# 104 gathered tokens spread over all partitions in place of 72, and 416 dense columns in place of 448, in a one-core decoder layer

## The reference

```
q = einsum('pd,dk->pk', xb, w_q)                 # 8 heads, two halves of 128
s = einsum('phcd,hcnd->phcn', q, keys)
s1, i1 = top_k(s[:, :, 0], 16); s2, i2 = top_k(s[:, :, 1], 16)
cand = s1[..., :, None] + s2[..., None, :]       # 16 x 16 for each head
top_s, top_pos = top_k(cand, 16)                 # 16 experts for each head
gate = softmax(top_s)                            # 8 x 16 = 128 gates for each token
a = gelu(einsum('pd,ped->pe', xb, u_tab[eidx]))
out = einsum('pe,ped->pd', gate * a, v_tab[eidx])
```

## Time and profile before

| | us |
|---|---|
| three runs | 2015.57, 2026.8, 2033.81 |
| median | 2026.8 |
| the profiled execution, its own time | 2021.1 |
| its span | 2018.5 |
| PE busy / POOL busy / DVE busy / ACT busy | 1891.0 / 1240.6 / 1114.7 / 607.5 |
| mean granted clock of TensorE | 0.967 |

### The profile page before, as it was taken

How to read it: one execution, slowest core, us unless ns; L and a number is a source line. 1 busy time by engine, 2 the same in 40 slices (tenths; PEclk the granted TensorE clock), 3 DMA queues, 4 the chain that set the end, 5 groups by cost and what they waited for, 6 DMA issues and landing times.

```text
span 2018.5 us, 31683 instructions
## 1 busy us (share of the span) xinstructions
PE 1891.0 (94%) x12867; PEld 1784.1 (88%) x12867; DVE 1114.7 (55%) x2280; ACT 607.5 (30%) x770; POOL 1240.6 (61%) x668
## 2 busy tenths in 40 slices
PE   5999996999999999999899999999899989889996
PEld 4889864969999999999899999998888888879896
DVE  4622646176477466667832122256576666567676
ACT  5212322232233323233332222232222223223232
POOL 0230100003777888888888887368888888888850
PEclk9999997999999999999999999999999999989997
DMA  7422395574356575766576666777878878878781
GB/s 259 177 84 95 110 345 156 178 246 141 64 127 143 113 156 100 154 123 131 120 186 141 143 138 134 215 243 242 256 219 260 242 226 253 241 214 271 234 240 48
DMA packets 210418, 361.75 MB, mean 179 GB/s; under 512 B 93969, under 2 KB 143121, under 8 KB 203233
## 3 DMA queue, kind: packets, MB, share of 16 engines
q1 hardware_dynamic: 136096, 318.76, 49.1%
q0 software_dynamic: 74176, 40.97, 15.2%
HBM read 291.45 MB, written 68.16 MB: 178 GB/s over the span
## 4 chain that ended last, share of the span: by engine, by line
PE 36%; POOL 21%; DVE 7%; issue 6%; DMA 3%; ACT 0%; another core or an unknown queue 0%; DVEq 0%; SPq 0%; ACTq 0%
PE ps L1469 29%; POOL ag L1637 12%; POOL qp L1644 9%; PE ps L1492 6%; DMA qp<-vtab,row 3%; DVE ul L1680 1%; PE ps L1455 1%; PE ps L1434 1%; DVE topi L135 0%; DVE h L214 0%; DVE h L228 0%; DVE h L223 0%; DVE pick L218 0%; DVE pick L235 0%; DVE h L207 0%
## 5 line engine op out<-in xcount | busy, mean ns | idle before, releaser
L100 POOL DMA_INDIRECT gates_dram<-gate,where x384 | 655.4, 1707 | 335.5 <-DVE where L254 193.0
L1492 PE MATMUL ps<-cl,uh 128*128 128x448 f32 x1024 | 380.2, 371 | 44.2 <-DVE ul L1680 43.3
L1469 PE MATMUL ps<-hl,uh 128*128 128x260 f32 x2048 | 415.7, 284 | 2.3 <-DVE ul L1680 2.3
L1469 PE MATMUL ps<-hh,ul 128*128 128x260 f32 x2048 | 414.0, 284 | 0.0
L1469 PE MATMUL ps<-hh,uh 128*128 128x260 f32 x2048 | 413.2, 283 | 0.0
L1492 PE MATMUL ps<-ch,ul 128*128 128x448 f32 x1024 | 377.6, 369 | 0.0
L1492 PE MATMUL ps<-ch,uh 128*128 128x448 f32 x1024 | 377.2, 368 | 0.0
L1680 DVE TENSOR_TENSOR ul<-us,uh 128x1024 fp32r<-128x1024 f32 x132 | 161.2, 1224 | 351.8 <-issue 244.2
L1637 POOL DMA_INDIRECT ag<-ahead_dram,where x128 | 275.5, 2153 | 72.8 <-issue 38.8
L1469 PEld LDWEIGHTS ps<-hl,uh 128*128 128x128 f32 x2048 | 316.9, 189 | 3.2 <-DVE ul L1680 2.9
L1469 PEld LDWEIGHTS ps<-hh,ul 128*128 128x128 f32 x2048 | 316.9, 189 | 0.0
(11 more groups left out here) (222 smaller groups left out, 2341.7 us busy)
## 6 DMA issues: line engine op xcount, KB each, us to landing
us<-utab SPq DMA_DIRECT2D x128, 512.0 KB
pairs<-vtab SPq DMA_DIRECT2D x124, 512.0 KB
ahead_dram<-a SPq DMA_DIRECT2D x128, 224.0 KB
qp<-ahead_dram SPq DMA_DIRECT2D x64, 448.0 KB
gt<-gates_dram SPq DMA_DIRECT2D x64, 448.0 KB
wr<-w_ada SPq DMA_DIRECT2D x24, 1024.0 KB, 6.0
gates_dram<-blank SPq DMA_DIRECT2D x24, 1024.0 KB, 8.8
wr<-w_in SPq DMA_DIRECT2D x14, 1024.0 KB, 4.8
```

Source lines behind the costliest of these rows:

```text
L100: nc.gpsimd.indirect_dma_start(out=io["gates"].rearrange("g p c a t -> (g p c a t)").unsqueeze(1), out_offset=bass.IndirectOffsetOnAxis(ap ...
L1469: last = nc.tensor.matmul(out[:, half, :], w, r[:, k, half * TH:(half + 1) * TH], start=(k == 0 and q == 0), stop=(k == KD - 1 and q == 2))
L1492: last = nc.tensor.matmul(ps[:, k, 0:ND], w, r[:, n % NL, :], start=(n == 0 and q == 0), stop=(n == NK - 1 and q == 2))
```

## The change

- The last tile begins at 416: `EDGES` is 0, 128, 256, 384, 416, 520. So `ND` is 416, `TG` is 104, and the fourth tile has 32 tokens in place of 64.
- A gathered token's 128 experts are spread over several partitions. The 104 tokens are three groups: the last 8 tokens (the samples) over 16 partitions each, 32 tokens over 4 each, 64 tokens over 2 each. Every group fills 128 partitions, with 8, 32 and 64 choices for each partition, 104 choices in all. There are therefore 104 pairs of indirect DMAs with 128 rows in place of 128 pairs with 72 rows, and 104 sums of 128 x 1024.
- The offsets, rows and gates of the last tile are brought into that layout through DRAM: SP writes them with nine strided DMAs (`pack`, ahead of block 85 of the first stage) and reads them back with one (`packed_back`); GpSimd waits for it ahead of its gathers.
- `fg` has three parts, one for each group. The samples' part is folded from 128 partitions to 8 by four pairs of a DMA on SP and an addition on DVE (`fold`, at blocks 30 to 44). The partial sums of the two prompt groups are added by 8 products each with a 0/1 matrix (`gathered_sums`, float32) right into the columns 416 to 511 of the eight banks, after blocks 70 and 126. The first product of each bank is 512 wide to clear them.
- `GCH`, the number of activations fetched ahead, is 8 in place of 16. `summed` now places the last sum at block 123.
- The samples' squares and norm move from the end into blocks 46 and 50. Behind the last block the norm and the residual run over 512 columns in place of 448, and the separate pieces for the 64 gathered prompt tokens go.

```diff
-EDGES = (0, 128, 256, 384, 448, T)
+EDGES = (0, 128, 256, 384, 416, T)
...
+GROUPS = ((96, 8), (64, 32), (0, 64))
...
-    TD = ND // 4
+    TD = SEQ // 4
...
-    GCH = 16
+    GCH = 8
...
+    GROUP_AT = [sum(n for _, n in GROUPS[:g]) for g in range(len(GROUPS) + 1)]
+    PACK_AT, PACKED_AT = 84, 88
+    FOLDS = (64, 32, 16, 8)
+    FOLD_AT, FOLD_EVERY = 30, 4
+    SAMPLES_AT = FOLD_AT + FOLD_EVERY * len(FOLDS)
+    TURN_AT = 70
...
-        return 0 if n < G0 else min(HK, -(-(n - G0 + 1) * HK // (NK - G0 - 1)))
+        return 0 if n < G0 else min(TG, -(-(n - G0 + 1) * TG // (NK - G0 - 4)))
...
+                def pack():
+
+                    sp.wait_ge(pick_ok, picked(TILES - 1))
+                    for a_, src in enumerate((where[:, TILES - 1].bitcast(F32), row[:].bitcast(F32),
+                                              gate[:, TILES - 1])):
+                        for g, (first, n) in enumerate(GROUPS):
+                            sp.dma_start(packing[a_].rearrange("(h t) s -> t h s", t=n)
+                                         [:, :, GROUP_AT[g]:GROUP_AT[g + 1]],
+                                         src[first:first + n].rearrange("t (h s) -> t h s", s=n))\
+                                .then_inc(packed_out, 16)
...
+                def gathered_sums(g):
+
+                    first, n = GROUPS[g]
+                    pe.wait_ge(fg_ok, GROUP_AT[g + 1])
+                    pe.wait_ge(chosen_ok, 1)
+                    for k in range(KD):
+                        nc.tensor.matmul(ps[:, k, ND + first:ND + first + n], fg[:, g, k * P:(k + 1) * P],
+                                         chosen[:, first:first + n], start=False, stop=False)
...
+                            whole = n == 0 and q == 0
+                            columns = slice(0, SEQ if whole else ND)
+                            last = nc.tensor.matmul(ps[:, k, columns], w, r[:, n % NL, columns],
+                                                    start=whole, stop=(n == NK - 1 and q == 2))
...
-                pool.wait_ge(pick_ok, picked(TILES - 1))
+                pool.wait_ge(packed_in, 16)
                 pool.wait_ge(g_ok, BATCHES)
                 for m in range(NK - NA, NK):
                     pool.wait_ge(*stored(m))
-                for r in range(-GCH, HK):
-                    if r + GCH < HK:
+                for r in range(-GCH, TG):
+                    if r + GCH < TG:
                         at = r + GCH
                         nc.gpsimd.indirect_dma_start(
                             out=ag[:, at:at + 1], out_offset=None, in_=words,
-                            in_offset=bass.IndirectOffsetOnAxis(ap=where[0:TG, TILES - 1, at:at + 1], axis=0))\
+                            in_offset=bass.IndirectOffsetOnAxis(ap=packed_choice[:, 0, at:at + 1].bitcast(U32), axis=0))\
                             .then_inc(ag_in[at // GCH], 16)
...
                         nc.gpsimd.indirect_dma_start(
                             out=vg[:, r % NG, :], out_offset=None, in_=values,
-                            in_offset=bass.IndirectOffsetOnAxis(ap=row[0:TG, r:r + 1], axis=0))\
+                            in_offset=bass.IndirectOffsetOnAxis(ap=packed_choice[:, 1, r:r + 1].bitcast(U32), axis=0))\
                             .then_inc(vg_in[r % NG], 16)
...
-                    nc.vector.scalar_tensor_tensor(fg[:], vg[:, r % NG, :], ag[:, r:r + 1], fg[:],
+                    sums_of = fg[:, group_of(r), :]
+                    nc.vector.scalar_tensor_tensor(sums_of, vg[:, r % NG, :], ag[:, r:r + 1], sums_of,
                                                    ALU.mult, ALU.add).then_inc(fg_ok, 1)
+
+                def fold(n):
+
+                    w = FOLDS[n]
+                    dve.wait_ge(fold_in, 16 * (n + 1))
+                    nc.vector.tensor_tensor(fg[0:w, 0, :], fg[0:w, 0, :], folded[0:w], ALU.add).then_inc(fold_ok, 1)
```

More of the change, by code:

```diff
@@ L44 @@
 NGRP = NK // GB
-AHEAD = NK
+AHEAD = NK + 1
 CLEARS = 24
@@ L1244, in summed, with group_of @@
     def summed(n):
-        return 0 if n < G0 else min(HK, -(-(n - G0 + 1) * HK // (NK - G0 - 1)))
+        return 0 if n < G0 else min(TG, -(-(n - G0 + 1) * TG // (NK - G0 - 4)))
+    def group_of(r):
+        return next(g for g in range(len(GROUPS)) if r < GROUP_AT[g + 1])
     stack, early = ExitStack(), ExitStack()
@@ L1313, in peer_stage @@
         cl_ok = sem("cl_ok")
-        ag_in = [sem(f"ag_in{n}") for n in range(HK // GCH)]
+        ag_in = [sem(f"ag_in{n}") for n in range(TG // GCH)]
+        packed_out, packed_in = sem("packed_out"), sem("packed_in")
+        fold_in, fold_ok, chosen_ok = sem("fold_in"), sem("fold_ok"), sem("chosen_ok")
         vg_in = [sem(f"vg_in{n}") for n in range(NG)]
@@ L1381, in coefficients @@
                             sp.wait_ge(scattered[i], 16 * HK)
-                        for c in range(2):
-                            sp.wait_ge(kept[c], 16 * (ST // CH // 2))
+                        for c in range(ST // CH):
+                            sp.wait_ge(kept[c % 2], 16 * (c // 2 + 1))
                     if q >= NV:
@@ L1497, in _ @@
                         last.then_inc(w_mm, 1)
+                    if n == TURN_AT:
+                        gathered_sums(1)
+                    if n == NK - 2:
+                        gathered_sums(2)
                 pe.wait_ge(fn_ok, 1)
-                pe.wait_ge(f_ok, 2)
-                pe.wait_ge(fsq_ok, 2)
+                pe.wait_ge(f_ok, 1)
+                pe.wait_ge(fsq_ok, 1)
                 for k in range(KD):
[L1503 to L1506, removed]
+                    last = nc.tensor.transpose(ps[:, 0, k * NS:(k + 1) * NS], sample_rows[:, k * P:(k + 1) * P],
+                                               ident[0:NS, 0:NS])
                 last.then_inc(ft_mm, 1)
                 pe.wait_ge(sum_ok, 1)
-                pe.wait_ge(fs_ok, 1)
-                for c in range(ND // TD):
+                pe.wait_ge(f_ok, 2)
+                for c in range(SEQ // TD):
                     last = nc.tensor.matmul(ps[0:TD, 1, c:c + 1], squares[:, 0, c * TD:(c + 1) * TD], ones[:, 0:1],
@@ L1756, in _ @@
                     if n == 0:
-                        dve.wait_ge(kept[0], 16 * (ST // CH // 2))
-                        dve.wait_ge(kept[1], 16 * (ST // CH // 2))
+                        for c in range(ST // CH):
+                            dve.wait_ge(kept[c % 2], 16 * (c // 2 + 1))
                         coefficients(0)
                         coefficients(1)
+                        nc.vector.tensor_scalar(cl[:, 0, ND:SEQ], ident[:, 0:SEQ - ND], 0.0, None, ALU.mult)
                         low_coefficients(0)
-                        nc.vector.memset(fg[:], 0.0)
+                    if 0 < n <= len(GROUPS):
+                        nc.vector.memset(fg[:, n - 1], 0.0)
+                    if n == len(GROUPS) + 1:
+                        for first, columns in GROUPS[1:]:
+                            last = nc.vector.tensor_reduce(chosen[:, first:first + columns],
+                                                           ident.rearrange("p (h t) -> p t h", t=columns), AX.X,
+                                                           ALU.add)
+                        last.then_inc(chosen_ok, 1)
                     if 0 <= n < NK - LEAD:
```

105 lines of the change are left out of this document (65 added, 40 removed).

## The result

| us | before | after |
|---|---|---|
| median, beside each other on one chip | 2022.3 (2015.57 to 2033.81) | 1917.49 (1916.59 to 1918.47) |
| ratio, 95% interval | | 0.9476 (0.9428 to 0.9525) |
| span of the profiled execution | 2018.5 | 1914.8 |
| first stage ends | 1315.3 | 1305.1 |
| second stage, to the end of its last product | 680.5 | 587.5 |

The kernel is 5.2% faster; 1.2% slower was forecast. The spans differ by 103.7 us: 10.2 less ahead of the second stage, 93.0 less in it, 0.5 less behind it.

What follows compares the result with a forecast made beforehand. It took gathers, admitted only in DVE's pauses, to set the second stage's pace, not PE. First stage -10, second stage +34, 0/1 products +2 on 2021.1 gave 2047; plus 5.7 to the median, stated as 2052, range 1966 to 2114.

Steps and rivals of the forecast that it cites:

- First stage, -10: First stage: halving the fourth tile's 16 batches saves 7 us, and a late batch that goes saves 3.
- PE's pace, 0.1864 a product: Second stage: 416 columns take 0.1864 us a product, 4.48 a block for 4.80, 41 us less if PE sets the pace.
- rival C: Second stage: PE stays the bound and DVE's gap does not matter, 128 x 4.48 us; total 1921, chance 0.07.
- The gather of 128 rows at 1.55 us: GpSimd, second stage: a 128-row gather takes 1.55 us, taken from the scatter, between bounds 0.94 and 1.67.
- rival B: Second stage: rows nearly free on GpSimd, 0.94 us a gather, 5.7 us a sum; total 1983, chance 0.20.
- The gap of 1.06 us: Second stage: at PE's new pace DVE's idle gap in a block with a sum is 1.06 us.
- One DMA passes, not 1.79: Second stage: indirect DMAs get on only in DVE's gaps; one passes a block where 1.79 are needed.
- the 87 sums at 6.5 us: Second stage: once the lead is used up, 87 sums wait for rows at 6.5 us each, 566 us in all.
- The number of DMAs a block: Second stage: the indirect DMAs needed a block fall from 2.15 to 1.79.
- Rival B's bytes, 5.2 us a block at 271 GB/s: Second stage: DMA engines must move 1.42 MB a block, allowing no faster than 5.2 us a block, 5.8 a sum.
- Rival D: Second stage: GpSimd keeps DVE out for a whole 128-row gather, at least 7.4 us a sum; total 2130, chance 0.06.
- 0/1 products, 2: PE, second stage: 16 products with the 0/1 matrices, half in DVE's shadow and half on the path, add 2 us.

Runs made afterwards that it cites:

- e12: Kernel before with 104 of its 128 sums (72 partitions) and 416 columns in all second-stage blocks but first and last: 1925.28 us, ratio 0.953.
- e8: Kernel before with only the second stage narrowed to 416 columns, first and last block excepted; 128 sums over 72 partitions: 2015.32 us, ratio 0.9977.
- e7: Kernel before with only 104 of its 128 sums and their gathers done; 72 partitions, 448 columns: 1959.39 us, ratio 0.9715.
- e4: Kernel before with its DVE sums over 128 partitions in place of 72 (extra weights 0), gathers still 72 rows: 1962.3 us, ratio 0.9696.
- e11: Kernel before with its 128 sums over 128 partitions and 416 columns in all blocks but first and last; 72-row gathers: 1952.15 us, ratio 0.9642.
- e14: Kernel before with 128 sums over 128 partitions, 416 columns in inner blocks, and v_tab gathers of 128 rows: 1920.39 us, ratio 0.9497.

## Why the prediction was wrong, step by step

- **First stage, -10:** right, 10.2.
- **PE's pace, 0.1864 a product:** 2% too fast. From 1631.01 on, 56 blocks took 255.37 us, 0.190 a product and 4.56 a block in place of 4.48. The 0.200 for 448 columns was read from two starts; over the last 480 products of the kernel before it is 97.87/480 = 0.204. For the whole stage rival C had 573 + 10 = 583, and it took 587.5.
- **The gather of 128 rows at 1.55 us:** wrong, 0.94. The scatter of the earlier trace rows was the nearest row and the wrong kind of row. In the forecast's own sum it is worth 69 us (2052 against rival B's 1983), about half of the miss; the other 66 are the next step but one. No run has a gather of 1.55, so what that would have cost with the gate as it is stays open.
- **The gap of 1.06 us:** right (1.05 in e12).
- **"One DMA passes, not 1.79":** this is the step that failed, and the forecast held it for a gather of 0.94 us too. It rests on "an indirect DMA gets on only when DVE pauses", which was false: a DMA can get in between two DVE instructions that follow back to back, and the trace of before has cases (the DMA of 1422.61 above). In e12 a second DMA that starts just behind the gap, while DVE is in `cl`, gets in at the end of `cl`; in the changed kernel 81 of the 87 that stand behind the coefficients get in there, with no gap either. Two pass in a block, so "PE's pace can therefore not be held" falls, and with it the 10 blocks of lead and the 87 sums at 6.5 us: 715 for the second stage, where 587.5 came and DVE waited for no row.
- **The number of DMAs a block:** the forecast had it, 2.15 to 1.79, and gave it too little. The room at PE's pace is near two: e8, which needs more, gains nothing from its columns; e7, which needs less, gains 58 us. A GpSimd that has fallen behind gets less, as most of its DMAs that stand long are held (32 of 36 at the boundary behind `cl`).
- **The sum, 1.28 us at either width:** right for DVE. That its width decides about GpSimd's DMAs was in no step. It is a second way to the same gain (e4), which the changed kernel has but does not need.
- **Rival B's bytes, 5.2 us a block at 271 GB/s:** wrong as a ceiling. That rate belonged to gathers of 72 rows (e11 sits on it, 32 us above e14); with 128 the engines moved 313 to 344. Whether a row's time to landing L stayed as it was, no wait after shows: DVE waits for none.
- **Rival D:** falls; no gather kept DVE out, and e14's DVE does 128 wide sums at PE's pace.
- **0/1 products, 2:** 1.71 and 1.73, 3.4 in all, as both turns lie on the path. **Behind the last block, 0 within 2:** right, 0.5 less.

Both reasons against rival C, the second DMA that starts too late and the bytes, were drawn from stretches in another regime: held DMAs that had stood for long, and DMA engines loaded by 72 rows. That made 0.07 of the case whose time, 1921, came within 4 us. Its condition, 1.79 DMAs in each gap, was not met and not needed: they also get in outside the gap.

The gain taken apart, by the ratios: 58 us come from fewer sums (e7), 37 from fewer columns once the rows are on time (e12 against e7), and 10 from the first stage, 105 together, which is what lies between the medians. The first is known to some 10 us either way, the second to some 15 (e12's four runs lie between 1923.8 and 1940.7), so the close agreement of the sum is partly luck.

## What to carry to other kernels

Where two resources take turns as the bound, price a change by demand against capacity for each block (here 2.15 and 1.75 DMAs against two), and ask first on which side of the step it lands: the same 32 columns were worth nothing measurable on one side and 37 us on the other. A rule of blocking read from a few long waits must be counted over all waits of the trace, the short ones too, before a forecast rests on it: here the trace of before already held cases against the rule. Try 128 partitions, or another multiple of 32, for a VectorE instruction that runs beside GpSimd's DMAs, and 128 for the rows of a gather; neither cost anything on its engine here, and they gave 60 and 32 us in the kernels here that were bound by them.

## What the hardware showed unexpectedly

- The partition count of one VectorE instruction (72, 80, 104 against 64, 96, 128) changes whether an indirect DMA gets in between two others: 0 of 91 against 50 of 60 and 84 of 95. In the time: 2030.5 against 1962.3 for 72 and 128, at the same length of the instruction. But 104, where another boundary opens, comes to 1972.3.
- An indirect gather that nothing keeps out holds GpSimd for 0.94 us, be it 72 or 128 rows, 4 bytes or 4 KB a row. The scatter of 128 values takes 1.55.
- 72-row gathers raise the time that the other DMA traffic holds the engines by 18% (68.3 against 58.1% for 106 MB); 77% more bytes on the gathers' queue (52.41 against 29.55 MB) lowered the share of all between 1340 and 1600 us from 0.93 to 0.90.
